# MoE decoder step: experts ranked by token count on chip, the 48 largest one to a step, the 16 smallest two to a step in 64-column lanes, with four weight buffers

## The reference

```python
x = x + W_out[ mLSTM heads | causal pooling heads ](rmsnorm(x) @ w_in)
# MoE on all 576 tokens: 64 experts, each token in 8 of them
scores = sigmoid(x @ router_w)                       # top 8 within the top 4 of 8 groups
gates  = scores of the chosen / their sum * 2.5
hb     = silu(x @ ex_w1[e]) * (x @ ex_w3[e])         # ex_w1, ex_w3: 1024 x 256
routed = sum over e of (hb * gate[e]) @ ex_w2[e]     # ex_w2: 256 x 1024
x = x + routed + shared_expert(x)
x = x + (p @ w_ple_proj) * sigmoid(rmsnorm(x) @ w_ple_gate)
y = rmsnorm(x)
```

## Time and profile before

| what | us |
|---|---|
| median of three runs | 1162.27 |
| profiled execution, its own time | 1161.14 |
| its span, first to last instruction | 1159.2 |
| PE busy | 1118.2 |
| DVE busy | 484.7 |
| ACT busy | 175.8 |
| POOL busy | 423.7 |

### The profile page before, as it was taken

How to read it: one execution, slowest core, us unless ns; L and a number is a source line. 1 busy time by engine, 2 the same in 40 slices (tenths; PEclk the granted TensorE clock), 3 DMA queues, 4 the chain that set the end, 5 groups by cost and what they waited for, 6 DMA issues and landing times.

```text
span 1159.2 us, 11979 instructions
## 1 busy us (share of the span) xinstructions
PE 1118.2 (96%) x3688; PEld 559.7 (48%) x3688; DVE 484.7 (42%) x1359; ACT 175.8 (15%) x429; POOL 423.7 (37%) x477
## 2 busy tenths in 40 slices
PE   6999999899998999999999999999999999998796
PEld 4777455555544444444444444444444444443342
DVE  4201223455596334434433433443443343343884
ACT  4110033110211101111110110111111011012222
POOL 5000411110205354455445445444544544542221
PEclk9999999999999999999999999999999999999899
DMA  9021250320594889999999999999999999974931
GB/s 286 29 57 71 73 151 1 109 64 37 180 358 141 312 331 355 341 350 352 362 332 353 348 346 361 355 345 357 344 349 343 347 353 336 351 280 122 425 145 73
DMA packets 89672, 296.34 MB, mean 256 GB/s; under 512 B 21818, under 2 KB 32250, under 8 KB 70949
## 3 DMA queue, kind: packets, MB, share of 16 engines
q1 hardware_dynamic: 67501, 258.14, 61.2%
q0 software_dynamic: 22144, 37.85, 9.0%
HBM read 285.99 MB, written 40.93 MB: 282 GB/s over the span
## 4 chain that ended last, share of the span: by engine, by line
PE 93%; DVE 2%; DMA 2%; issue 1%; ACT 1%; POOL 1%; SPq 0%; POOLq 0%; DVEq 0%; ACTq 0%
PE bank L1983 38%; PE bank L1646 22%; PE bank L1971 19%; PE bank L2025 5%; PE bank L1652 2%; PE bank L1992 1%; DMA arena<-y_dram 1%; PE bank L1732 1%; PE bank L1742 1%; PE bank L1779 1%; PE bank L1933 1%; PE bank L1641 1%; DMA x<-in_x_prompt 1%; PE bank L1873 0%; PE bank L1729 0%
## 5 line engine op out<-in xcount | busy, mean ns | idle before, releaser
L1983 PE MATMUL bank<-arena 128*128 128x512 f32 x1024 | 450.2, 592 | 1.1 <-DVE arena L1509 1.1
L766 POOL DMA_INDIRECT arena<-xs_dram,slot x268 | 280.8, 1048 | 344.5 <-DVE slot L1495 275.9
L1983 PEld LDWEIGHTS bank<-arena 128*128 128x128 f32 x1024 | 189.6, 190 | 216.2 <-issue 214.2
L1971 PE MATMUL bank<-arena 128*128 128x512 f32 x512 | 235.5, 603 | 0.9 <-ACT arena L982 0.9
L1971 PEld LDWEIGHTS bank<-arena 128*128 128x128 f32 x512 | 92.1, 190 | 92.9 <-issue 92.9
L1551 DVE SCALAR_TENSOR_TENSOR arena<-bank,gate,arena 128x256 f32<-128x256 f32 x64 | 31.0, 485 | 233.4 <-ACT arena L978 233.4
L1646 PE MATMUL bank<-xT,ring 128*128 128x288 f32 x384 | 93.4, 406 | 0.0
L978 ACT ACTIVATE arena<-bank 128x256 f32<-128x256 f32 x64 | 24.6, 384 | 398.9 <-PE bank L1983 398.9
L1546 DVE COPY outrow<-yrow 128x1 int32<-128x1 int32 x64 | 9.8, 154 | 179.0 <-PE bank L1971 179.0
L1509 DVE STREAM_TRANSPOSE arena<-arena 128x1024 f32<-128x1024 f32 x66 | 81.9, 1241 | 4.0 <-DMA arena<-xs_dram,slot 3.6
L1646 PEld LDWEIGHTS bank<-xT,ring 128*128 128x128 f32 x384 | 72.9, 190 | 20.5 <-issue 0.5
(11 more groups left out here) (326 smaller groups left out, 913.5 us busy)
## 6 DMA issues: line engine op xcount, KB each, us to landing
arena<-in_ex_w SPq DMA_DIRECT2D x192, 1024.0 KB, 8.3
arena<-y_dram SPq DMA_DIRECT2D x16, 1024.0 KB, 11.3
ring<-in_w_in SPq DMA_DIRECT2D x5, 2048.0 KB, 8.5
arena<-xs_dram,slot POOLq DMA_INDIRECT x268
ring<-in_w_out SPq DMA_DIRECT2D x2, 2048.0 KB, 8.5
ring<-in_w_ple_gate SPq DMA_DIRECT2D x2, 2048.0 KB, 24.4
x<-in_x_prompt SPq DMA_DIRECT2D x4, 512.0 KB, 6.5
arena<-in_state_C SPq DMA_DIRECT2D x8, 256.0 KB, 6.4
```

The source lines that it names most:

```text
L766: pool.indirect_dma_start(xg[b][:, 256 * a:256 * a + 256], None, xs_quarter, bass.IndirectOffsetOnAxis(slot[k][:, a:a + 1], 0), bounds_che ...
L1971: ins = pe.matmul(bank[5 + half][:, :], hT[:, c, :], w2s[b][:, c, 512 * half:512 * half + 512], start=(c == 0), stop=(c == 1))
L1983: ins = pe.matmul(bank[2][:, :], xgT[b][:, c, :], w13[b][:, :, wc, :], start=(c == 0), stop=(c == KT - 1))
```

## The change

- The experts are ranked by token count on the chip. The rank is found on VectorE and put in order by a small product ("ord") on TensorE; `order` in SBUF holds the experts' numbers, and every engine that needs one reads it into a register (`value_load`).
- 64 experts are put into 56 steps: of every seven steps, six have one of the 48 largest experts, the seventh has two of the 16 smallest. In a pair step each matmul of the two products becomes two, on 64 columns of the array each; the one-hot and pick work is done for both experts.
- Fourteen steps are unrolled (two periods), once ahead of the loop and once in a loop of three turns.
- Four weight buffers: the ring's two halves, `mixpj` and two homes in the arena. Loads 0 and 2 start once the order is known, loads 1 and 3 after the shared expert, load m from then on when the first product of load m - 4 is done.
- The w_ple_gate chunks, which share the ring, are loaded at the end of the loop.
- `passes` is also raised if the 49th largest count does not fit 64 columns.
- Splitting the gates into three bf16 parts moves from VectorE to GpSimd; "pos" comes earlier in TensorE's order.

```diff
+    PAIRS = 8
+    PERIOD = NE // PAIRS - 1
+    STEPS = PAIRS * PERIOD
+    UNROLL = 2 * PERIOD
+    LOADS = 2 * (PERIOD + 1)
+    TURNS = STEPS // UNROLL
...
+        w13 = [ring[:, 0, :], mixpj[:, 0:WORDS]] + [t[:, 0:WORDS] for t in homes]
...
+        def is_pair(j):
+
+            return j % PERIOD == PERIOD - 1
+
+        def first_load(j):
+
+            return j // PERIOD * (PERIOD + 1) + j % PERIOD
...
+            sp.wait_ge(s_order, 2)
+            for m in (0, 2):
+                e = expert(m)
+                load13(m, e)
+                load2(m, e)
...
+            after(sp, "y", NT - 1, 0)
+            wait_drained(sp, "pT", NT - 1)
+            for m in (1, 3):
+                e = expert(m)
+                load13(m, e)
+                load2(m, e)
...
+            with sp.Fori(0, passes * TURNS - 1) as turn:
+                held = expert(sp.snap((turn * LOADS + (LOADS - 1)) % NE))
+                for i in range(LOADS):
+                    e = expert(sp.snap((turn * LOADS + (LOADS + i)) % NE))
+                    sp.wait_ge(s_mm1, turn * UNROLL + (UNROLL + step_of(i - 4) + 1))
+                    load13(i % 4, e)
+                    sp.wait_ge(s_mm2, turn * UNROLL + (UNROLL + step_of(i - 5) + 1))
+                    load2((i - 1) % 4, held)
+                    held = e
...
+            sp.wait_ge(s_mm1, more * STEPS + (STEPS - 2))
+            load_chunk("gt1")
+            sp.wait_ge(s_mm2, more * STEPS + (STEPS - 1))
+            load_chunk("gt0")
...
+            def one_hot_pair(at, pair, b, e0, e1):
+
+                dve.tensor_copy(cols[b], table[:, bass.ds(e0, 1), :].rearrange("p a c -> p (a c)")
+                                ).then_inc(s_cols, 1)
+                dve.tensor_copy(colsx, table[:, bass.ds(e1, 1), :].rearrange("p a c -> p (a c)")
+                                ).then_inc(s_colx, 1)
...
+            pe.wait_ge(s_order, 1)
+            b = free_bank(pe, "ord")
+            pe.matmul(b[0:1, 0:NE], ids, hits, start=True, stop=True)
+            pe.matmul(b[0:1, NE:2 * NE], key_col, hits, start=True, stop=True).then_inc(filled, 1)
             second(1)
...
+                        if is_pair(j):
+                            for lane in range(2):
+                                t = slice(NS * lane, NS * lane + NS)
+                                ins = pe.matmul(bank[2][t, :], xgT[b][:, c, t], w13[(m + lane) % 4][:, :, wc, :],
+                                                start=(c == 0), stop=(c == KT - 1))
+                        else:
+                            ins = pe.matmul(bank[2][:, :], xgT[b][:, c, :], w13[m % 4][:, :, wc, :], start=(c == 0),
+                                            stop=(c == KT - 1))
```

More of the change, by code:

```diff
@@ L280, in decoder_step @@
         top = ex(NT * K).rearrange("p (i k) -> p i k", k=K)
+        ids, key_col, rank_col = (ex(1)[0:NE, :] for _ in range(3))
+        revs = ex(NE)[0:NE, :]
         sh_at = anat_at - 2 * KT * FF
@@ L682, in _ @@
                 pool.memset(iotaq[:, c:c + 1], float(c))
+            for c in range(2):
+                pool.memset(iotap[:, c:c + 1], float(c))
             link(pool.memset(diagq[:, :], 1.0))
@@ L1535, in _ @@
             add_x("y", 4)
+            for k in range(AHEAD):
+                row = table[:, bass.ds(heads[k], 1), :]
+                dve.tensor_copy(table[:, NE + k:NE + k + 1, 0:NT], row[:, :, 0:NT])
+                dve.tensor_scalar(table[:, NE + k:NE + k + 1, NT:2 * NT], row[:, :, NT:2 * NT], -4.0, None, ALU.add)
+                dve.tensor_copy(table[:, NE + k:NE + k + 1, 2 * NT:NC], row[:, :, 2 * NT:NC])
             dve.wait_ge(s_np, 1)
@@ L1547, in out, with step @@
                     dve.tensor_copy(og[b][:, 512:DM], bank[6][:, :]).then_inc(s_out1, 1)
-                def step(n, j, first=False):
-                    dve.wait_ge(s_silu, r * NE + n + (j + 1))
-                    dve.scalar_tensor_tensor(out=hh, in0=bank[2][:, FF:2 * FF], scalar=gate[j][:, 0:1], in1=hs,
-                                             op0=ALU.mult, op1=ALU.mult).then_inc(s_h, 1)
+                def step(base, half, rows, pairs, load, j, first=False):
+                    dve.wait_ge(s_silu, base + (j + 1))
+                    dve.scalar_tensor_tensor(out=hh, in0=bank[2][:, FF:2 * FF], scalar=gate[j % PERIOD][:, 0:1],
+                                             in1=hs, op0=ALU.mult, op1=ALU.mult).then_inc(s_h, 1)
@@ new lines, in step @@
+                    index(base + (j + 4), (j + 3) % PERIOD, bank[7], lambda ins: None)
+                    turned_rows(rows + (j // 2 + 2) * 64, j % 2)
+                    m = load + first_load(j + 4)
+                    if is_pair(j + 4):
+                        e0, e1 = expert(m), expert(m + 1)
+                        one_hot_pair(base + (j + 5), pairs + ((j + 4) // PERIOD + 1), j % 2, e0, e1)
+                    else:
+                        one_hot(base + (j + 5), j % 2, expert(m))
+                for j in range(UNROLL):
+                    step(r * STEPS, r * (STEPS * 8), r * (STEPS * 32), r * PAIRS, 0, j, j == 0)
@@ new lines, in _ @@
+                with dve.Fori(1, TURNS) as n:
+                    for j in range(UNROLL):
+                        step(r * STEPS + n * UNROLL, r * (STEPS * 8) + n * (UNROLL * 8),
+                             r * (STEPS * 32) + n * (UNROLL * 32), r * PAIRS + n * 2, n * LOADS, j)
+                out(r * STEPS + STEPS, r * (STEPS * 8) + STEPS * 8, 0)
+                dve.wait_ge(s_onehot, r * STEPS + (STEPS + 4))
+                dve.tensor_scalar(iotaq[:, :], iotaq[:, :], 4.0, None, ALU.add).then_inc(s_place, 1)
@@ L1914, in _ @@
             second(0)
-            turn_h(1)
-            first(3)
             pe.wait_ge(s_sel0, 2)
@@ L1941, in _ @@
             first_pick(0)
+            turn_h(2)
+            first(4)
             second(2)
```

349 lines of the change are left out of this document (215 added, 134 removed).

## The result

The changed kernel takes 1094.07 us (median of 4 runs, 1091.38 to 1095.09) beside 1162.63 us for the kernel before on the same chip: ratio 0.9406, 95% interval 0.9394 to 0.9418, 68.6 us less. Run once more, beside the last of the experiments, it took 1092.98 us, ratio 0.9388 (0.9375 to 0.9401). The forecast was 1089 us in a range of 1078 to 1123. The profiled execution took 1095.09 us, its span is 1093.3 us. Lines 2150 and 2153 are now the first product (pair, single), 2132 and 2135 the second.

What follows compares the result with a forecast made beforehand. TensorE was taken as the bound, with DMA a close second. From the profiled execution, 1161.1 - 85.9 + 4.4 + 4 + 1 + 3 = 1087.6 us; the median, 1.1 us above, gave 1089 us, range 1078 to 1123.

Steps and rivals of the forecast that it cites:

- Fewer steps: Expert loop: eight of 64 steps disappear at 10.733 us each, 85.9 us less on TensorE's path.
- the pair step: Two-expert steps: two 64-column lanes cost what one full product costs; extras 0.55 us each, 4.4 us, bounds 0 and 16.
- serial lanes: Two-expert steps: lanes with different stationary tiles run one after the other, 82 us more, sum 1171 us; chance 0.04.
- the second pass: Whole loop runs twice if the 49th largest count exceeds 64, some 610 us more, about 1700 us; chance 0.03.
- the ceiling near 345 GB/s: Weight traffic in the loop: sustained DMA cannot rise above the old loop's rate; 1110 to 1157 us, named 1134; chance 0.06.
- VectorE in a step: Two-expert steps: second one-hot set (1.28 us) and two register reads stay hidden; taken as 0, up to 17 us.
- Longer loops: Fourteen unrolled steps: two jumps back may wait for code fetch, 0 to 4.8 us each, taken as 2, together 4 us.
- Before the loop: Ranking ahead of the loop: only added matmuls and four register reads count, 1 us, bounds -2 and 5.
- The first loads: Loop's start: loads 0 to 3 wait for routing or the shared expert; cost 0, up to 5 us if late.
- The gate weights: Loop's end: two 2 MB loads moved there fit into nearly empty DMA time; cost 0, up to 5 us.
- Feeding it: Expert weights in the loop: 396 GB/s needed, 397 taken as available, losing nothing; 3 us added for single late loads.
- the feed sets the pace: Loop: weights arrive at 371 to 380 GB/s, TensorE waits at pairs; costs 8 to 24 us, named 1104 us; chance 0.22.

Runs made afterwards that it cites:

- both edits: Changed kernel with one of eight row blocks of the first product left out and, from load 4 on, only half of each expert's w3 loaded: 1047.77 us, ratio 0.9007.
- early loads: Changed kernel with weight buffers renumbered so that loads 0, 1 and 2 are all issued once the order is known: 1091.41 us, ratio 0.9387.
- the block left out: Changed kernel with one of the eight row blocks of the first product left out in every step, all transfers kept: 1094.88 us, ratio 0.9415.
- the last version: Changed kernel with loads 0, 1, 2 issued early, projection matrix loaded behind the last expert's weights, first four register reads just ahead of use: 1090.82 us, ratio 0.9376.

## Why the prediction was right, and where not

*Fewer steps and the pair step* stood as worked out: 10.73 us a step, and 0.59 us for a pair where 0.55 were given. The step that carried the forecast, that two lanes cost what one full product costs, held with two stationary tiles as well. The rival of serial lanes is out, and so are the second pass (56 steps) and the ceiling near 345 GB/s.

*VectorE in a step*: cost nothing, as taken. The register reads are hidden.

*Longer loops*: 4 us given, nothing measured on TensorE. The page counts 22 instruction transfers on q8 and 32 on q14 (16 and 11 before, for q8), and some came while the loop turned. A window of the changed kernel's DMA queues, columns as in the earlier trace rows:

```profile
q1 hardware_dynamic: 24683, 138.85, 82.9%
q0 software_dynamic: 13060, 26.39, 16.9%
q14 instruction: 16, 0.13, 0.1%
q8 instruction: 5, 0.08, 0.1%
```

The code was fetched in the loop, in 460 to 880 us, and TensorE's pitch doesn't show it. VectorE does: behind its two jumps back its next instruction comes after 5.8 and 5.6 us, with a transfer on q14 in between, where it comes after 0.2 to 0.3 us in the kernel before and in those without pairs. The other engines go on within 0.3 us. So the scaled product of step 28 (L1684) begins 2.0 us behind ScalarE's SiLU, and not at once as at step 27. TensorE isn't held by it, because the second product of the step before still keeps it busy. In the kernel with both edits the same operation is 4.5 us late at step 42, and TensorE waits. VectorE in the changed kernel, steps 27 and 28, then VectorE and TensorE in the kernel with both edits:

```profile
666.91 0.48 DVE L1684 SCALAR_TENSOR_TENSOR arena<-bank,gate,arena 128x256 f32<-128x256 f32 x1 [3.47 <-issue]
679.71 0.48 DVE L1684 SCALAR_TENSOR_TENSOR arena<-bank,gate,arena 128x256 f32<-128x256 f32 x1 [5.30 <-issue]
...
799.49 0.48 DVE L1684 SCALAR_TENSOR_TENSOR arena<-bank,gate,arena 128x256 f32<-128x256 f32 x1 [5.23 <-issue]
800.03 0.44 PE L2163 MATMUL bank<-ident,arena 128*128 128x128 f32 x2 [1.77 <-DVE arena L1684]
```

So the term's mechanism held: the long body does wait at its jumps, on VectorE, and for longer than the 4.8 us of its bound. What failed is that this wait lies on the path. The prediction read the queue q8 alone; the one instruction transfer that the earlier trace rows have in the old loop is on q14, and so are those at VectorE's jumps. The Trainium skill (Runtime: NRT & Kernel Launch, Instruction fetch mechanics) has a taken branch outside its two lines wait for a fetch; VectorE's two jumps agree, and the other engines' show no such wait.

*Before the loop*: 1 us given, 4.6 measured; the sentence that failed is that "VectorE's order is covered there". Late routing made TensorE wait for VectorE: 1.7 us ahead of the counts (L1524) and 1.2 ahead of the first pick (L1613), both in the list of waits above. Another 1.7 us of the profiled execution are a lowered clock far ahead of the change, in 217 to 226 us:

```profile
217.00:226.00 9.00, 8.81 (x18) 3.95 (x19) 1.38 (x4) 0.00 (x0) 0.00 (x0) 0.81 0.01 2
```

The profile of the kernel before has 1.00 there. Where it was 1.00 in that stretch, in the changed kernel's second profile, the loop began at 365.3, 2.9 us later than before.

*The first loads*: "cost 0, and up to 5 if either is late". Load 1 was late, 2.8 us with the lowered clock behind it: issued at 366.5 us, half a microsecond ahead of the first product, it landed at 376.4, where some 7 us from its start were given; load 3 and the second matrices, issued by 369.8, were in the queue with it.

*The gate weights* were hidden. The chain of the changed kernel, answering to the last of the earlier trace rows:

```profile
991.91 11.05 DMA arena<-y_dram
```

This read of y begins 24.84 us after the last first product (967.07), 24.70 before (1036.25). The 3.3 us at the end are mostly the 2.5 us that pairs bring behind the last operation; I had no term for that.

*Feeding it* is the term that was mis-sized most. The break-even of 9.65 us an expert was right, and so was TensorE's need of 396 GB/s. But I took 397 GB/s "as filled and between the two loop values", which loses nothing. By the prediction's own count the service came to (966.3 - 364.5) / 61.7 = 9.75 us, 0.1 us over break-even; that is close to the 9.79 us of its lower value, 380 GB/s, of which it said "the end is 8 us late". The late waits cost 4.9 us, and a growing wait at the pairs is what it had named as the sign of the feed. So the forecast's mechanism held for five pairs, and that of the rival "the feed sets the pace" shows at the sixth and seventh, at less than its 8 to 24 us; the eighth had 0.8 us of lead. By bytes the rate was 393 GB/s, which at 3.72 MB an expert would be 9.47 us, 3% less than by landings. The trace accounts for the difference: while loads 11 to 54 landed, q1 moved 138.82 MB, the weights of 44.1 experts (3.146 MB each), for 43 that landed. More transfers were under way at the end of the stretch than at its start, each partly done. So by bytes the feed was short by less than 1% of TensorE's need; most of the lead went into transfers that were begun and not yet finished. Why more of them were under way isn't shown. The Trainium skill (DMA: Bandwidth & Descriptors, Where 436 GB/s comes from) lets some 358 GB/s of HBM bind; one core held 393 GB/s here for 500 us, gathers and scatters among them, and the measurement decides.

Against 1087.6 us for the profiled execution, then, the terms that missed are -4 (jumps), +3.6 (before the loop), +4.7 (feed) and +3.3 (end), 7.6 us together where 7.5 are to be explained: the direction and size were right for the stated reason, and the last 5 us of the way to TensorE's pace are the feed's. That the sum came so near is in part luck: the 4 us given to jumps, which cost TensorE nothing, paid for a third of the 11.6 us that the other three lacked.

## What to carry to other kernels

When an edit shortens the busiest engine, work out what the next resource must then deliver, and follow its lead from step to step, not only to the last transfer: here the lead of some 15 us that four buffers hold hid landings that came 3% too slowly for five pairs, and the wait showed at the sixth. Where two resources meet, relieve each by itself (leave out work, leave out bytes): 48 us less of TensorE's work changed nothing, 14% fewer bytes gave 5.4 us, and both together 46. A transfer that is only put ahead of another, with the queue full, buys nothing at the end; bytes taken out of the queue can. A pitch that doesn't change shows only that the pacing engine didn't wait: VectorE's 5.8 us at a jump stayed hidden until TensorE's step was shortened.

## What was not expected of the hardware

- A product that follows a wait of 1 to 3 us ran at a lowered granted clock (0.87 to 0.91 in windows of 13 and 14 us) and took 1.6 to 2 us longer. So a wait of 1.0 us cost 2.8 in all and one of 2.9 us 4.5. Not every one does: behind the wait of 1.7 us at step 41 of the kernel with early loads the product ran at full speed.
- The DMA engines at a share of 0.99 to 1.00 gave 393 to 394 GB/s over 420 to 500 us in four kernels (the changed one, early loads, the block left out, the last version), whether TensorE waited or not; with less asked of them, 341 to 365.
- Instruction transfers while a loop turned (5 and 16 in 420 us) cost TensorE no visible time; VectorE's two jumps back in the changed kernel took 5.8 and 5.6 us, and 0.2 to 0.3 in the kernels without pairs.
- GpSimd's closing DRAIN took 7.3 us in every kernel with pairs and 2.0 in the others, 2.5 us of the program's end.
